# Merge, output and query projections of a hybrid decoder block: loops written out, PSUM waits by bank, transposes two units into the next block, gates double-buffered

## The reference, cut to what matters

```
# y_gla: (256, 1024), y_nsa: (256, 2048); ga, gb: (256, 2048), columns of the input projection
m   = sigmoid(ga) * (y_gla @ w_up_gla) + sigmoid(gb) * (y_nsa @ w_up_nsa)
x1  = x + m @ w_out
xn  = rmsnorm(x1, norm2_g)
qp  = xn @ peer_w_q                      # (256, 8 heads * 128)
s1, s2 = scores of the halves of qp against sub_k1, sub_k2 of each head
```

## Time and profile before

| what | us |
|---|---|
| median of 3 runs | 2573.32 (2573.13 to 2574.76) |
| span of the profiled execution, first to last instruction | 2571.0 |
| PE busy | 2469.6 (96%) |
| DVE busy | 1503.7 (58%) |
| ACT busy | 1140.6 (44%) |
| POOL busy | 145.4 (6%) |
| chain that ended last: PE / DVE / ACT | 85% / 8% / 3% |

### The profile page before, as it was taken

How to read it: one execution, slowest core, us unless ns; L and a number is a source line. 1 busy time by engine, 2 the same in 40 slices (tenths; PEclk the granted TensorE clock), 3 DMA queues, 4 the chain that set the end, 5 groups by cost and what they waited for, 6 DMA issues and landing times.

```text
span 2571.0 us, 38713 instructions
## 1 busy us (share of the span) xinstructions
PE 2469.6 (96%) x14430; PEld 2185.9 (85%) x14430; DVE 1503.7 (58%) x2035; ACT 1140.6 (44%) x1013; POOL 145.4 (6%) x151
## 2 busy tenths in 40 slices
PE   7899978999999898999999999999999999999997
PEld 6788866788877778999999999999988888888885
DVE  5434466655545444588888866664545555555554
ACT  5434455444444333455455554544434443434342
POOL 0001054200000000000000000000000000000000
PEclk9899999999999999999999999999999999999999
DMA  7655644444445644465566565556676667676762
GB/s 268 229 176 218 220 154 141 174 149 156 150 180 209 228 152 175 161 201 200 193 215 207 201 240 213 206 222 243 223 258 243 248 237 250 231 258 228 254 236 99
DMA packets 84661, 530.12 MB, mean 206 GB/s; under 512 B 9856, under 2 KB 10112, under 8 KB 30448
## 3 DMA queue, kind: packets, MB, share of 16 engines
q1 hardware_dynamic: 58464, 423.65, 46.1%
q0 software_dynamic: 14896, 59.12, 6.7%
q10 hardware_dynamic: 11232, 46.37, 4.4%
HBM read 480.87 MB, written 48.23 MB: 206 GB/s over the span
## 4 chain that ended last, share of the span: by engine, by line
PE 85%; DVE 8%; issue 4%; ACT 3%; DMA 0%; ACTq 0%; DVEq 0%; POOL 0%; POOLq 0%
PE psum L1079 9%; PE psum L1081 9%; PE psum L1080 9%; PE psum L725 9%; PE psum L727 9%; PE psum L726 9%; PE psum L1028 7%; PE psum L1027 7%; PE psum L1029 7%; DVE w_lo L1126 2%; PE psum L1055 2%; ACT w_hi L402 1%; PE psum L862 1%; PE psum L782 1%; PE psum L983 1%
## 5 line engine op out<-in xcount | busy, mean ns | idle before, releaser
L1126 DVE TENSOR_TENSOR w_lo<-w_raw,w_hi 128x2048 fp32r<-128x2048 f32 x400 | 920.9, 2307 | 678.0 <-ACT w_hi L402 668.8
L402 ACT ACTIVATE w_hi<-w_raw 128x2048 fp32r<-128x2048 f32 x400 | 763.8, 1913 | 686.4 <-DMA w_raw<-in_w_units 472.6
L1027 PE MATMUL psum<-ynT_hi,w_hi 128*128 128x256 f32 x2048 | 581.2, 284 | 0.0
L1029 PE MATMUL psum<-ynT_lo,w_hi 128*128 128x256 f32 x2048 | 579.5, 283 | 0.0
L1028 PE MATMUL psum<-ynT_hi,w_lo 128*128 128x256 f32 x2048 | 579.5, 283 | 0.0
L1079 PE MATMUL psum<-w_hi,w_up 128*128 128x512 f32 x1024 | 399.2, 390 | 4.4 <-issue 4.4
L1080 PE MATMUL psum<-w_lo,w_up 128*128 128x512 f32 x1024 | 398.9, 390 | 0.0
L1081 PE MATMUL psum<-w_hi,w_low 128*128 128x512 f32 x1024 | 398.8, 389 | 0.0
L1028 PEld LDWEIGHTS psum<-ynT_hi,w_lo 128*128 128x128 f32 x2048 | 393.1, 192 | 0.0
L1027 PEld LDWEIGHTS psum<-ynT_hi,w_hi 128*128 128x128 f32 x2048 | 393.1, 192 | 0.0
L1029 PEld LDWEIGHTS psum<-ynT_lo,w_hi 128*128 128x128 f32 x2048 | 393.0, 192 | 0.0
(11 more groups left out here) (303 smaller groups left out, 2365.4 us busy)
## 6 DMA issues: line engine op xcount, KB each, us to landing
w_raw<-in_w_units SPq DMA_DIRECT2D x400, 1024.0 KB, 4.8
hid_scratch<-hst ACTq DMA_DIRECT2D x32, 512.0 KB, 5.8
h_in<-hid_scratch POOLq DMA_DIRECT2D x16, 1024.0 KB, 5.5
g_tab<-tab_scratch POOLq DMA_DIRECT2D x16, 1024.0 KB, 11.3
proj_scratch<-evac ACTq DMA_DIRECT2D x24, 512.0 KB, 4.3
tab_scratch<-gate_a ACTq DMA_DIRECT2D x10, 1024.0 KB, 4.1
tab_scratch<-gate_b ACTq DMA_DIRECT2D x6, 1024.0 KB, 3.9
x_nat<-in_x POOLq DMA_DIRECT2D x2, 2048.0 KB, 8.5
```

The costliest lines, as they stand in the source:

```text
L402: act.activation(w_hi[:, s % SPLIT, :], w_raw[:, s % RAW, :], ACT.Copy).then_inc(hi_done, 1)
L1027: pe.matmul(out, uh, h2T_hi[:, c, :], start=c == 0, stop=False, skip_group_check=True)
L1029: ins = pe.matmul(out, uh, h2T_lo[:, c, :], start=False, stop=c == KC - 1, skip_group_check=True)
L1126: dve.tensor_tensor(w_lo[:, s % SPLIT, :], w_raw[:, s % RAW, :], w_hi[:, s % SPLIT, :].bitcast(F32), ALU.subtract).then_inc(lo_done, 1)
```

## The change

- All loops of the merge, output and query stages on PE, ACT, DVE and POOL are written out, with constants in the place of register values.
- Waits by bank: units on banks 0 and 1 of merge block nb wait for line 1360 of block nb-1, units on banks 2 and 3 for line 1364 of block nb-1. Output block 0 waits for line 1360 of merge block 3, output block 1 for line 1364 of merge block 3, and blocks 2 and 3 for line 1383 of block b-2. The query halves wait for line 1383 of output blocks 2 and 3.
- A transposed block is needed by one unit each in the next stage, so unit k of output block 0 waits only for merged block k, and query unit k of the first half only for output block k.
- All 8 transposes stand two units into the next block (that of merge block 3 in output block 0, that of output block 3 in the query stage), and the copies on ACT and DVE likewise.
- `gab` has two buffers with a semaphore each. The gates of blocks 0 and 1 are loaded at once, those of blocks 2 and 3 when the addition of block nb-2 is done.
- On ACT the square root of the norm (line 606) moves behind the first `hi` of the query stage; on DVE one `lo` moves ahead of the norm's arithmetic.

The diff, cut to its core:

```diff
-        region(AT_NSA, AT_X, ("gab", [P, 2, NT, NB]))
+        region(AT_NSA, AT_X, ("gab", [P, 2, 2, NT, NB]))
...
 POOL
-            with pool.Fori(0, 4) as nb:
-                wait_alone(pool, m_done, nb * 2 + FIRST)
+            for nb in range(4):
+                if nb >= 2:
+                    pool.wait_ge(m_done, 2 * (nb - 1) + M_FIRST)
                 for a, b in ((0, B_GA), (1, B_GB)):
-                    pool.dma_start(gab[:, a, :, :], proj[ds(nb + b, 1), :, :, :].rearrange("a p t n -> p (a t) n")).then_inc(gab_in, 16)
+                    pool.dma_start(gab[:, nb % 2, a, :, :], proj[nb + b]).then_inc(gab_in[nb % 2], 16)
...
 ACT, merge
+            for nb in range(4):
+                for k in range(6):
+                    if k == 2 and nb:
+                        merged_upper(nb - 1)
+                    n = base + nb * 6 + k + AHEAD
+                    hi(n, n % 4)
+                    if k == 0:
+                        act.wait_ge(gab_in[nb % 2], (nb // 2) * 32 + 32)
+                        act.activation(gab[:, nb % 2, :, :, :], gab[:, nb % 2, :, :, :], ACT.Sigmoid).then_inc(gab_sig, 1)
 ACT, output
+            for b in range(4):
+                for k in range(UPB):
+                    if k == 2:
+                        if b:
                             x_upper(b - 1)
+                        else:
+                            merged_upper(3)
+                    n = base + b * 4 + k + AHEAD
+                    hi(n, n % 4)
+                act.wait_ge(x1_done, b + 1)
...
 ACT, query
-            act.wait_ge(ms2_done, 1)
-            act.activation(stat[:, 10:12], stat[:, 8:10], ACT.Sqrt).then_inc(sq2_done, 1)
             for par in range(2):
                 for k in range(UPB):
+                    if (par, k) == (0, 1):
+                        act.wait_ge(ms2_done, 1)
+                        act.activation(stat[:, 10:12], stat[:, 8:10], ACT.Sqrt).then_inc(sq2_done, 1)
+                    if (par, k) == (0, 2):
+                        x_upper(3)
...
 PE, merge
-                        if nbp == 1 and k == 1:
-                            turn_merged(nb - 1)
-                        unit(i * 12 + (base + nbp * 6 + k), nbp * 6 + k, 0, ygT_hi, ygT_lo, 4 * k, k == 0, k == UPG - 1, (m_done, nb * 2 + FIRST))
+            for nb in range(4):
+                for k in range(UPG):
+                    n = base + nb * 6 + k
+                    unit(n, n, 0, ygT_hi, ygT_lo, 4 * k, k == 0, k == UPG - 1, (m_done, 2 * nb - 1 + M_FIRST))
+                if nb:
+                    turn_merged(nb - 1)
...
+                for k in range(UPB):
+                    n = base + nb * 6 + UPG + k
+                    unit(n, n, 1, ynT_hi, ynT_lo, 4 * k, k == 0, k == UPB - 1, (m_done, 2 * nb + M_FIRST))
 PE, output
-            pe.wait_ge(m_hi, 4 + FIRST)
-            pe.wait_ge(m_lo, 4 + FIRST)
+            for b in range(4):
+                for k in range(UPB):
+                    if k == 2:
+                        if b:
                             turn_x(b - 1)
+                        else:
+                            turn_merged(3)
+                    if b == 0:
+                        pe.wait_ge(m_hi, k + 1 + FIRST)
+                        pe.wait_ge(m_lo, k + 1 + FIRST)
+                    n = base + b * 4 + k
+                    free = (m_done, 7 + b + M_FIRST) if b < 2 else (x1_done, b - 1)
+                    unit(n, n, b % 2, mT_hi, mT_lo, 4 * k, k == 0, k == UPB - 1, free)
 PE, query
-            pe.wait_ge(x_hi, 4 + FIRST)
-            pe.wait_ge(x_lo, 4 + FIRST)
-            pe.wait_ge(x1_done, 4 + FIRST)
             for par in range(2):
                 for k in range(UPB):
+                    if (par, k) == (0, 2):
+                        turn_x(3)
+                    if par == 0:
+                        pe.wait_ge(x_hi, k + 1 + FIRST)
+                        pe.wait_ge(x_lo, k + 1 + FIRST)
+                    if k == 0:
+                        pe.wait_ge(x1_done, par + 3)
                     query_unit(par, k)
...
 DVE, merge
+            for nb in range(4):
+                for k in range(6):
+                    n = base + nb * 6 + k + 1
+                    g = gab[:, nb % 2, :, :, :]
+                    if k == 2 and nb:
+                        merged_lower(nb - 1)
+                    if k == UPG - 1:
+                        dve.wait_ge(gab_sig, nb + 1)
+                        dve.wait_ge(m_done, 2 * nb + M_FIRST)
+                        dve.wait_ge(unit_done, n)
+                        dve.tensor_tensor(mrg[:, 0, :, :], psum[:, 0:2, :], g[:, 0, :, :], ALU.mult).then_inc(m_done, 1)
...
+                    lo(n - 1 + AHEAD, (n - 1 + AHEAD) % 4)
...
 DVE, query
             lo(base + AHEAD, AHEAD)
+            lo(base + AHEAD + 1, (AHEAD + 1) % 4)
+            x_lower(3)
             dve.wait_ge(sq2_done, 1)
```

More of the change, by code:

```diff
@@ L56 @@
 FIRST = 1
+M_FIRST = 2
 KL_POOL = 5
@@ L561, in _, with merged_upper @@
             act.wait_ge(stored[1], 16 * PROJ_BLOCKS // 2)
[L562 to L573, removed]
+            def merged_upper(m):
+                act.wait_ge(mt_done, m + 1)
+                act.activation(mT_hi[:, 4 * m:4 * m + 4, :].rearrange("p c t -> p (c t)"), psum[:, 4:6, :].rearrange("p b n -> p (b n)"), ACT.Copy).then_inc(m_hi, 1)
@@ L576, in x_upper @@
+            for nb in range(4):
[7 more added lines that the diff above has]
+                        act.activation(gab[:, nb % 2, :, :, :], gab[:, nb % 2, :, :, :], ACT.Sigmoid).then_inc(gab_sig, 1)
             def x_upper(b):
                 act.wait_ge(xt_done, b + 1)
-                act.activation(h2T_hi[:, ds(b * 4, 4), :].rearrange("p c t -> p (c t)"), psum[:, 4:6, :].rearrange("p b n -> p (b n)"), ACT.Copy).then_inc(x_hi, 1)
+                act.activation(h2T_hi[:, 4 * b:4 * b + 4, :].rearrange("p c t -> p (c t)"), psum[:, 4:6, :].rearrange("p b n -> p (b n)"), ACT.Copy).then_inc(x_hi, 1)
@@ L580, in _ @@
             base = PROJ_BLOCKS * UPB + 4 * (UPG + UPB)
[L581 to L586, removed]
-                            x_upper(b - 1)
[L588 to L593, removed]
+            for b in range(4):
+                for k in range(UPB):
+                    if k == 2:
+                        if b:
+                            x_upper(b - 1)
+                        else:
[3 more added lines that the diff above has]
+                act.wait_ge(x1_done, b + 1)
+                for t in range(NT):
+                    act.activation(gab[:, 0, t, 0, :], x_nat[:, t, b * NB:(b + 1) * NB], ACT.Square, accum_out=sq_x1[:, t, b:b + 1]).then_inc(sq2, 1)
+                    act.wait_ge(sq2, b * 2 + t + 1)
@@ L951, in _ @@
                     pe.wait_ge(evac_done, 2 * PROJ_BLOCKS)
-                    for k in range(UPB):
-                        unit(i * 12 + (base + nbp * 6 + UPG + k), nbp * 6 + UPG + k, 1, ynT_hi, ynT_lo, 4 * k, k == 0, k == UPB - 1, (m_done, nb * 2 + FIRST))
-                turn_merged(nb)
+                for k in range(UPB):
+                    n = base + nb * 6 + UPG + k
+                    unit(n, n, 1, ynT_hi, ynT_lo, 4 * k, k == 0, k == UPB - 1, (m_done, 2 * nb + M_FIRST))
             base = PROJ_BLOCKS * UPB + 4 * (UPG + UPB)
-            pe.wait_ge(m_hi, 4 + FIRST)
-            pe.wait_ge(m_lo, 4 + FIRST)
[L960 to L964, removed]
-                            turn_x(b - 1)
-                        unit(i * 8 + (base + par * 4 + k), k, par, mT_hi, mT_lo, 4 * k, k == 0, k == UPB - 1, (x1_done, b + FIRST))
-                turn_x(b)
+            for b in range(4):
+                for k in range(UPB):
+                    if k == 2:
+                        if b:
+                            turn_x(b - 1)
+                        else:
+                            turn_merged(3)
[5 more added lines that the diff above has]
+                    unit(n, n, b % 2, mT_hi, mT_lo, 4 * k, k == 0, k == UPB - 1, free)
             base = PROJ_BLOCKS * UPB + 4 * (UPG + UPB) + 4 * UPB
@@ L1115, in _ @@
         def _(dve):
-            for s in (g_y, g_ylo, g_att, mx_done, o_lo, pt_v, m_done, m_lo, x1_done, x_lo):
+            for s in (g_y, g_ylo, g_att, mx_done, o_lo, pt_v, m_lo, x_lo):
                 dve.sem_inc(s, FIRST)
+            dve.sem_inc(m_done, M_FIRST)
             step = Steps(dve, v_step)
@@ L1350, in _ @@
             dve.wait_ge(stored[1], 16 * PROJ_BLOCKS // 2)
[L1351 to L1369, removed]
+            for nb in range(4):
[9 more added lines that the diff above has]
+                        dve.tensor_tensor(mrg[:, 0, :, :], psum[:, 0:2, :], g[:, 0, :, :], ALU.mult).then_inc(m_done, 1)
+                    if k == UPG + UPB - 1:
+                        dve.wait_ge(unit_done, n)
+                        step(dve.tensor_tensor(mrg[:, 1, :, :], psum[:, 2:4, :], g[:, 1, :, :], ALU.mult))
+                        dve.tensor_tensor(mrg[:, 1, :, :], mrg[:, 1, :, :], mrg[:, 0, :, :], ALU.add).then_inc(m_done, 1)
```

(23 more changed lines are left out.)

15 lines of the change are left out of this document (8 added, 7 removed).

## The result

| | before | after |
|---|---|---|
| median (runs) | 2574.04 us (4: 2573.13 to 2577.43) | 2534.74 us (4: 2532.20 to 2535.85) |
| profiled execution: span | 2571.0 | 2534.2 (its own time: 2535.85) |
| merge stage begins | 743.11 | 739.67 |
| first expert unit | 1057.65 | 1020.71 |
| the stretch between | 314.54 | 281.04 |

The ratio is 0.9842 with a 95% interval of 0.9828 to 0.9856: 1.6% faster. The forecast was 2538.7, its range 2537 to 2548.

What follows compares the result with a forecast made beforehand. PE was taken to bound the kernel, paying each pause as a wait and again at low clock. Span 2571.0 less 34.6 gives 2536.4; with the median 2.3 over the span, 2538.7 us, range 2537 to 2548.

Steps and rivals of the forecast that it cites:

- What bounds: Whole kernel: PE, busy for 96% of the span, sets the time; only its work and pauses count.
- The work that stays, 279.97: Merge stage to first expert unit: PE's work without removable pauses at full clock, 279.97 us against 314.54 now.
- Low clock, "that is 8.0": Merge, output and query stages: PE's time lost at low clock behind pauses, 8.0 us, would go.
- the two sums: Same stretch: gain of 34.6 us, counted from work that stays and from waits 25.0, low clock 8.0, restarts 1.5.
- The sum against the span, "2571.0 - 34.6": Whole kernel: the gain taken off the profiled span gives 2536.4 us.
- The 2.3: Whole kernel: the runs' median lies 2.3 us over the span, added to reach 2538.7.
- Gates, taken at 0: Fifth merge unit: second block's early gates load costs 0; 1.4 us wait if both blocks' gates came side by side.
- Weights under a PE that never pauses, 0: Merge and output stages: weight loads keep up with PE, gaining 1.6 us per pair of units; cost 0.
- rivals 1 and 2: Weight pipeline partly falls behind, 9 us, 2548, chance 0.08; weight landings grow when nothing pauses, 2577, chance 0.03.
- Copies behind the late transposes, code, square root, keys: 0: Output and query stages: late copies, moved square root, keys' load and removed register work make PE wait 0.
- rival 3: PE's instruction fetch: at most 4 more packets, each exposed by 2.7 us, 11 us, 2550; chance 0.03.
- Rival 4: All eight transposes in the stream lower PE's clock, 10 to 22 us, 2549 to 2561; chance 0.02.

Runs made afterwards that it cites:

- e6: The changed kernel with POOL's 1 MB load of the second norm's weights moved from before the gates to before the reload of x; 2533.72 us, ratio 0.9846.
- e1: The changed kernel once more, nothing altered; 2535.5 us, ratio 0.9851.
- e4: The changed kernel with the first units waiting again for the whole block before, transposes and copies still two units in; 2558.81 us, ratio 0.9942.
- e8: The changed kernel with one gates buffer, its load waiting for the addition of the block before; 2535.3 us, ratio 0.9844.
- e5: The kernel before with only ACT's merge loop written out; one run of 2577.45 us.
- e9: The kernel before with only POOL's loop over the gates written out; one run of 2574.46 us.
- e7: The kernel before once more, nothing altered; 2574.82 us, ratio 1.0004.

## Why the prediction missed, step by step

1. *What bounds.* Right. PE bounds the stretch before and after, and every wait the change was to remove is gone.
2. *The work that stays, 279.97.* Right to 0.3 us in e6, and to 1.1 in the changed kernel, where the wait of 1.3 more than covers the difference.
3. *Low clock, "that is 8.0".* This is the term that failed in the gain. It was read from one profile, which was the cheapest of six with these waits: the other five gave 12.0 to 13.4. The stretch was "34.6 us less" by that draw and is 38.5 us less against the 319.6 that is the median of the six. The medians say 39.3. That the two sums agreed at 34.6 was no check of this term, as both were read from the same profile.
4. *The sum against the span, "2571.0 - 34.6".* The absolute number failed here. That span held a cheap stretch but a late start: the stages in front took 743.11, the longest of twelve profiles, which lie from 736.60 to 743.11 (mean 740.3). The changed kernel's profile drew 739.67. Its run of 2535.85 stood 2.9 us under the forecast: 3.4 from this start and 0.65 from what lies around the span (2.3 assumed, 1.65 found), less the 1.1 by which the stretch was longer than forecast. The median lies 1.1 lower still. The 2.3 was itself mixed of two executions: on record each run of the kernel before lies 2.0 to 2.2 over its own span, each of the changed kernel 1.6 to 1.7. The stretch behind, untouched too, took 1513.3 to 1513.5 in seven profiles and 1514.2 to 1514.7 in five. The kernel before, in 15 runs of one chip beside e1 to e4, went from 2569.3 to 2578.9, while the three runs shown had spanned 1.6 us. The range allowed 1.7 us below the forecast, where the start alone spreads over 6.5, and no term of the sum had such a spread. The cheap stretch did not enter this sum, since its work was counted anew; the late start did.
5. *Gates, taken at 0.* Wrong in the choice. PE waited 1.3 and 1.5 us at the unit named, against a bound of 1.4. The bound's slack, 1.5 us from 14.3, was right: it is the 15.8 of the table. Its delay of 2.9 us was met by luck, as the mechanism given was wrong: it is not the second block's load (e8). The Trainium skill's rule that DMAs of one queue are not ordered (DMA: Bandwidth & Descriptors, section Two DMAs through the same engine are not ordered) was therefore not what decided. In the changed kernel's profile the four loads of the first two blocks landed in the order of their issue, at 13.3, 17.2, 18.3 and 19.7 us. What the runs show in its place: in the kernel before, ACT loads its table for 1.28 us ahead of the first `hi` of the stage, which then starts 6.3 us behind the start of the stage, against 4.8 once ACT's loop is written out (e5). The next weights are then issued 1.5 us earlier and run beside the second half of the gates. Taking 1 MB out in front of the gates cures it (e6); POOL's loop alone changes nothing (e9). What stays open is why the half landed at 15.9 with ACT's loop alone and at 16.4 to 17.4 with the others too; e5 is one profile.
6. *Weights under a PE that never pauses, 0.* Right. ACT's waits for `w_raw` rose from 67.4 us in the stretch of the kernel before to 116.9, and no wait of PE beyond the fifth unit came of them. The row of after (ACT, us in total, times, longest):

```profile
ACT w_hi L405 <- DMA w_raw<-in_w_units: 116.9, 29, 7.4
```

   The landing took 4.9 us in the median (4.8 in the earlier trace rows), at most 8.0, so rivals 1 and 2 did not come.
7. *Copies behind the late transposes, code, square root, keys: 0.* Right. No wait named them. Packets of instructions in the stretch rose from 7 to 12, one more than rival 3 had at most, with no idle time marked issue, so it is out.
8. *Transposes and the clock.* Rival 4 is out: 257.67 us at 1.00 with all eight transposes in the stream. Here the trace and the Trainium skill's sentence on transposes (TensorE: Matmul & The Clock Gate, Part 4) disagree for runs this short.

## What to carry to other kernels

The pauses of PE of 2.4 to 3.3 us cost more than their length here, and how much more differed from one execution to the next; price such a term from several profiles, or give it a spread. When the sum is set against one execution, the stages that the change does not touch bring their own draw: compare stretches, and let the range hold the spread of the whole. Wait for the bank that is written, and put the transposes where a unit or two cover them: neither alone removed the pauses, and each gave less than half of what both did.

## What was not expected of the hardware

The same instructions, behind pauses of the same length, met a falling clock in one execution and not in the next. Before the third and the fourth merge block the kernel before paused 2.6 us in the first profile and in e7 alike. The third ran below full clock in both, at 0.96 and 0.95. The fourth took 33.72 us in the first profile and 35.42 at 0.95 in e7. The row of the first profile:

```profile
852.66:886.38 33.72, 33.72 (x152) 27.78 (x152) 15.78 (x8) 11.77 (x7) 1.59 (x3) 1.00 0.73 274
```

The Trainium skill (TensorE: Matmul & The Clock Gate, section What's actually happening) says that the gate watches PE in windows that run free of the kernel; the spread seen here agrees with that.

Writing the loops out removed three of ACT's five table loads of 1.28 us in these stages, one of them at the entrance of the merge loop, though no activation in the source had changed. A loop written out on ACT for the sake of order thus moved a load of weights by 1.5 us, and with it the gates.
